# One decoder step on one Trainium2 core: factor sums of the gate and up weights kept in DRAM, sums of the down weights on VectorE, other queues for some transfers

## The chip, the cores and the metric

One core of a Trainium2 chip runs the whole program. The metric is the device time of one execution in microseconds: 2733.95 us is the median of 3 runs (2731.45 to 2736.58).

## The reference

One layer of a hybrid decoder, all in fp32, over 2048 prompt rows and 32 sample rows of width 1024. The change touches only its last part, the feed-forward network:

```python
h2 = rms_norm(x1, norm2_g) * (1.0 + scale2) + shift2
ff = (silu(h2 @ w_gate) * (h2 @ w_up)) @ w_down      # w_gate, w_up: 1024 x 2816, w_down: 2816 x 1024
y = x1 + gate2 * ff
```

Ahead of it come the modulation, the input projection, a dilated attention, a state space and the output projection. Two more outputs are the key and value caches of the 8 samples, moved on by 4 positions: 16 copies of 2044 rows of 2 KB from DRAM to DRAM, one for each cache and sample.

## The kernel before

**How a product is made.** All of the network is in `ffn_parts` (L2473). Each matrix product is done by Strassen's method in Winograd's form: a product of 2x2 quarters as 7 products of sums of quarters instead of 8. For fp32 accuracy each operand is split into a high part (rounded to fp32r, a copy on ScalarE) and a low part (the rest, a subtraction on VectorE), and three matmuls take high x high, high x low and low x high.

**The order of the work on TensorE.** The 2048 rows go in 4 blocks of 512 (`FB`; block 2 also takes the 32 sample rows). In a block, 11 pairs (`NPAIRS`) of column tiles of gate and up weights are taken one after the other, each with 7 products (`PRODUCTS`) of 2 x 12 matmuls (L2860): 1848 matmuls in a block. After blocks 1 and 3 comes the down projection of the last two blocks: 7 products of 11 pieces of 12 matmuls (L2902), 924 matmuls. So the order is block 0, block 1, down 0, block 2, block 3, down 1. In block 3 the 8 matmuls of `sample_parts(n)` (L2872) for the sample rows stand behind product 3 of every pair.

**How weights come in.** SyncE (SP) issues the loads in `load_raw` into a ring of 8 tiles of 128 x 1024 (512 KB, `RAWS`). In a pair of a block there are 4 such tiles, the quarters A21, A22, A11, A12 of the pair's gate and up weights, in packets of 512 bytes. VectorE makes the 4 sums of the pair from them, in place and in `s1` (`weight_sum`, through L3053 and L3045), and does so in all 4 blocks anew. For each product ScalarE (`fill_hi`, L2961) and VectorE (`fill_lo`, L3045) fill one of 4 slots (`SLOTS`) of split weights; slot s+4 is filled once TensorE has let go of slot s. In the down projection a ring tile holds one piece: 512 columns of activation sums (`aF`) and 512 of a weight or weight sum (`w_down`, `wF`). A ring tile is loaded again when the slot made from it is filled (`raw_freed`).

**What GpSimd (POOL) does.** `pool_part` walks through the pairs, waiting for each pair's last product (L3125, L3127 of VectorE). It issues one copy of a cache (`move`, L2731 and L2732) in pairs 1, 4, 6 and 9 of every block. Over blocks 0 and 1 it loads the quarters of `w_down` (`load_quarters`, L2750), makes their 4 sums (`t_sum`, L2746) and stores them (`wF`, L2767), one tile k in 2 pairs. In block 3 it loads the quarters for `sample_parts` into the one buffer `wq`. In blocks 0 and 2 it makes the 4 sums of the next block's activations (L2774). In the down projections it loads rows of `x1` and stores rows of `y_prompt` (`y_dma`, L2742).

**What ScalarE and VectorE do besides.** ScalarE copies product banks out (L2978) and takes SiLU (L2990). VectorE adds products up (L3108), multiplies (L3125) and forms the sums of the activations (`stage_sums`, L3133), which SP stores to `aF` (L2671).

The queue of POOL's transfers is q0, that of SP's and ScalarE's is q1.

Of the kernel before, what the change touches and what calls it, by code (L numbers as in the profile page):

```python
# [7 lines left out]
ALU = mybir.AluOpType  # L8
# [2457 lines left out]
ROUND_RAWS = 2 * PAIR_RAWS * NPAIRS + PIECES  # L2466
# [6 lines left out]
def ffn_parts(nc, t, const, P, M, sig):  # L2473
# [10 lines left out]
    Y_BUF = {C11: 1, C22: 0, C21: 1, C12: 0}  # L2484
    T_AT = {2: 0, 3: 3, 4: 1, 5: 2}
# [3 lines left out]

    def raw_of(b, n, x):  # L2490
        return b // 2 * ROUND_RAWS + (b % 2 * NPAIRS + n) * PAIR_RAWS + x

    def raw_of_piece(r, p, k):
        return r * ROUND_RAWS + 2 * NPAIRS * PAIR_RAWS + p * DEPTH + k

# [5 lines left out]

    def raw_at_index(i):
        r, i = divmod(i, ROUND_RAWS)
        if i < 2 * NPAIRS * PAIR_RAWS:
            g, x = divmod(i, PAIR_RAWS)
            return "pair", 2 * r + g // NPAIRS, g % NPAIRS, x
        return ("piece", r) + divmod(i - 2 * NPAIRS * PAIR_RAWS, DEPTH)
# [55 lines left out]
    s1 = M.at("f_s1", [128, 1024], M.held + 73728)  # L2563
# [6 lines left out]
    wq = M.at("f_wq", [128, 4, 512], M.early + 24576)  # L2570
# [21 lines left out]
    staged, down_copied, wq_moved, t_summed = (P.sem("f_" + v) for v in ("staged", "down_copied", "wq_moved", "t_summed"))  # L2592
# [17 lines left out]

    def load_raw(sp, i):
        dst = raws[i % RAWS]
        kind, *at = raw_at_index(i)
        if kind == "pair":
            _, n, x = at
            k0, col = x % 2 * (KT // 2), (2 * n + (1 if x in (A21, A22) else 0)) * 128
# [32 lines left out]
    def sp_part(sp):  # L2649
# [10 lines left out]
        def raw_freed(i):  # L2660
            kind, *at = raw_at_index(i)
            if kind == "pair":
                b, n, x = at
                sp.wait_ge(w_lo, slot_of(b, n, (4, 5, 3, 6)[x]) + 1)
            else:
                sp.wait_ge(w_lo, slot_of_piece(*at) + 1)

# [13 lines left out]
        def main():  # L2681
# [3 lines left out]
            for i in range(RAW, ROUNDS * ROUND_RAWS):  # L2685
                kind, *at = raw_at_index(i)
# [4 lines left out]
                if kind == "piece":  # L2691
                    r, p, k = at
                    if p == 0:
                        sums_stored(sp, (2 * r + 1) * NPAIRS + k + 1)
                    if p == min(T_AT) and r == 0 and k == 0:
                        sp.wait_ge(wq_moved, 32 * DEPTH)
                load_raw(sp, i)
                if kind == "pair":
                    b, n, x = at
                    if x == A12:  # L2700
                        if b % 2 * NPAIRS + n >= 3:
                            store_sums(b * NPAIRS + n - 3)
                        if b % 2 == 0 and n == 3:
                            load_next(b + 1)
                else:
                    last = (2 * r + 2) * NPAIRS - 1
                    if p == 0 and k in (3, 7, 9):
                        store_sums(last - {3: 2, 7: 1, 9: 0}[k])
# [17 lines left out]
    def pool_part(pool):  # L2726
# [706 lines left out]
```

## Time and profile before

| | |
|---|---|
| median of 3 runs | 2733.95 us |
| profiled execution | 2731.9 us |
| its span, first to last instruction | 2730.1 us |
| mean granted TensorE clock | 0.974 |
| PE, DVE, ACT, POOL busy | 94%, 73%, 47%, 19% |
| moved by the DMA engines | 583.52 MB, mean 214 GB/s |

The network runs from 1284 us to the end. A granted clock of 1.00 is 2.4 GHz, the other level is 1.2 GHz, and a figure between them is a mean over a stretch. The DMA share is the busy time of packets over that of 16 engines; since packets overlap it can be above 1. A copy from DRAM to DRAM counts once in GB/s.

### The profile page before, as it was taken

To read this page: it belongs to the slowest core of one execution; us is meant where nothing else is said; L and a number is where in the kernel's file an instruction comes from. 1 tells how busy PE (TensorE), PEld (TensorE's weight loads), DVE (VectorE), ACT (ScalarE), POOL (GpSimd) and SP (SyncE) were. 2 spreads that over 40 slices of the span, in tenths; PEclk is the share of its full clock that TensorE was granted. 3 is DMA by queue.
4 is the path that set the end of the run, shared out by engine and by line. 5 is a ranking of instruction groups with operands and counts; after the bars stand their busy time and mean duration, and the time that the engine had idled before them with its cause. 6 is when DMAs were issued, how large, how long until landed. Compare 5 with 4: busy or idle time off the path is not lost.

```text
span 2730.1 us, 46745 instructions
## 1 busy us (share of the span) xinstructions
PE 2575.6 (94%) x17757; PEld 2214.9 (81%) x17757; DVE 1983.1 (73%) x3672; ACT 1285.1 (47%) x2509; POOL 507.8 (19%) x632
## 2 busy tenths in 40 slices
PE   5999999999999999998999899989999998888998
PEld 3678887777787778787999899978899997787787
DVE  6657886567767468677999999837698996665546
ACT  4221222247889465665554554535445553443443
POOL 2107787430001000000223121200000100000000
PEclk8999999999999999999999999999999999998999
DMA  9663334753433985445898789787777767766774
GB/s 331 204 191 114 128 119 136 283 175 125 127 110 120 386 320 194 156 151 166 272 312 261 225 266 294 270 273 230 237 218 231 226 195 226 228 210 230 228 225 158
DMA packets 407081, 583.52 MB, mean 214 GB/s; under 512 B 35105, under 2 KB 295969, under 8 KB 396866
## 3 DMA queue, kind: packets, MB, share of 16 engines
q1 hardware_dynamic: 380152, 428.96, 48.9%
q0 software_dynamic: 24256, 150.70, 16.4%
q8 instruction: 142, 2.33, 0.4%
q10 hardware_dynamic: 2450, 0.87, 0.1%
q14 instruction: 81, 0.66, 0.1%
HBM read 447.76 MB, written 199.27 MB: 237 GB/s over the span
## 4 chain that ended last, share of the span: by engine, by line
PE 59%; DVE 8%; DMA 4%; ACT 3%; issue 3%; SPq 1%; POOL 0%; DVEq 0%; ACTq 0%
PE f_ps L2860 23%; PE f_ps L2902 14%; PE c_ps_w L2165 6%; DMA f_wq<-in_w_down_dram 3%; PE a_o_ps L406 2%; PE a_s_ps L377 2%; DVE f_ws L3045 2%; PE a_t_ps L388 2%; PE c_ps_glu L2140 2%; PE b_ps_t L1787 1%; ACT a_probs L444 1%; PE a_o_ps L414 1%; PE b_ps_o L1824 1%; PE b_ps_s L1799 1%; DVE f_s L3053 1%
## 5 line engine op out<-in xcount | busy, mean ns | idle before, releaser
L2860 PEld LDWEIGHTS f_ps<-f_x,f_ws 128*128 128x128 f32 x7392 | 905.2, 191 | 52.1 <-issue 46.1
L2860 PE MATMUL f_ps<-f_x,f_ws 128*128 128x256 f32 (+1 forms) x7392 | 910.7, 286 | 35.6 <-DVE f_sl L3108 22.4
L2902 PE MATMUL f_ps<-f_ws 128*128 128x512 f32 x1848 | 422.9, 391 | 10.6 <-DVE f_ws L3045 10.6
L2902 PEld LDWEIGHTS f_ps<-f_ws 128*128 128x128 f32 x1848 | 347.9, 189 | 85.8 <-DVE f_ws L3045 11.9
L946 PE MATMUL p_out_ps<-p_w,p_hT 128*128 128x512 f32 x1620 | 380.0, 392 | 1.3 <-DVE p_qk L1222 1.1
L946 PEld LDWEIGHTS p_out_ps<-p_w,p_hT 128*128 128x128 f32 x1620 | 300.8, 188 | 73.5 <-issue 11.6
L3045 DVE TENSOR_TENSOR f_ws<-f_raw,f_ws 128x1024 fp32r<-128x1024 f32 x208 | 269.2, 1300 | 124.1 <-ACT f_ws L2961 123.8
L3045 DVE TENSOR_TENSOR f_ws<-raw,f_ws 128x1024 fp32r<-128x1024 f32 x210 | 262.9, 1257 | 115.9 <-ACT f_ws L2961 115.5
L2961 ACT ACTIVATE f_ws<-raw 128x1024 fp32r<-128x1024 f32 x210 | 220.9, 1057 | 208.5 <-PE f_ps L2902 111.2
L2961 ACT ACTIVATE f_ws<-f_raw 128x1024 fp32r<-128x1024 f32 x208 | 218.8, 1057 | 210.8 <-PE f_ps L2902 103.5
L2978 ACT ACTIVATE f_us<-f_ps 128x256 f32<-128x256 f32 (+1 forms) x264 | 100.0, 384 | 205.4 <-PE f_ps L2860 203.6
L444 ACT ACTIVATE a_probs<-a_probs,a_o 128x256 f32<-128x256 f32 (+1 forms) x384 | 171.1, 451 | 1.9 <-DVE a_o L487 1.9
L487 DVE CUSTOM_DVE_ANT_0 a_probs<-a_s_ps,a_mask 128x256 f32<-128x256 f32 (+1 forms) x384 | 117.8, 364 | 60.1 <-issue 59.1
L2165 PE MATMUL c_ps_w<-c_wout_h,c_mT 128*128 128x512 f32 (+1 forms) x544 | 130.8, 397 | 1.8 <-ACT c_mT L2269 1.8
L2165 PEld LDWEIGHTS c_ps_w<-c_wout_h,c_mT 128*128 128x128 f32 (+1 forms) x544 | 98.6, 184 | 27.6 <-ACT c_mT L2269 2.3
L2746 POOL TENSOR_TENSOR f_wq<-f_wq 128x512 f32<-128x512 f32 x44 | 84.4, 1929 | 135.3 <-DVE f_stage L3125 97.7
L863 ACT ACTIVATE p_qk<-p_out_ps 128x1024 f32<-128x1024 f32 (+1 forms) x17 | 17.4, 1024 | 172.4 <-PE p_out_ps L946 172.4
L2990 ACT ACTIVATE f_sl<-f_sl 128x256 f32<-128x256 f32 (+1 forms) x132 | 54.9, 416 | 83.4 <-DVE f_sl L3108 82.3
L3108 DVE TENSOR_TENSOR f_sl<-f_ps,f_us 128x256 f32<-128x256 f32 (+1 forms) x132 | 55.4, 420 | 51.3 <-ACT f_us L2978 51.3
L406 PE MATMUL a_o_ps<-a_probsT,a_v 128*64 128x128 f32 x1200 | 86.7, 281 | 0.2 <-DVE a_probsT L470 0.2
L1216 DVE TENSOR_REDUCE p_hss<-p_qk 128x16 f32<-128x1024 f32 (+1 forms) x17 | 20.7, 1219 | 87.6 <-ACT p_qk L863 87.4
L388 PE MATMUL a_t_ps<-ident,a_probs 128*128 128x128 f32 x600 | 83.9, 277 | 0.2 <-ACT a_probsT L437 0.2
(381 smaller groups left out, 3769.1 us busy)
## 6 DMA issues: line engine op xcount, KB each, us to landing
scratch_aF<-f_stage SPq DMA_DIRECT2D x44, 896.0 KB, 6.6
out_dram<-in_cache_k_dram POOLq DMA_DIRECT2D x8, 4088.0 KB, 14.6
out_dram<-in_cache_v_dram POOLq DMA_DIRECT2D x8, 4088.0 KB, 14.4
raw<-in_w_gate_dram SPq DMA_DIRECT2D x88, 256.0 KB, 5.1
raw<-in_w_up_dram SPq DMA_DIRECT2D x88, 256.0 KB, 5.4
f_raw<-in_w_gate_dram SPq DMA_DIRECT2D x88, 256.0 KB, 4.7
f_raw<-in_w_up_dram SPq DMA_DIRECT2D x88, 256.0 KB, 5.3
f_wq<-in_w_down_dram POOLq DMA_DIRECT2D x22, 1024.0 KB, 7.3
```

Source lines behind the costliest of these rows:

```text
L388: mm = pe.transpose(bank[:, c * QB:(c + 1) * QB], pr[:, n % 2, hd, b * QB:(b + 1) * QB], ident[:, :])
L406: mm = pe.matmul(o_ps[n % 2][e * HD:(e + 1) * HD, pair * QB:(pair + 1) * QB], v[:, (n - (blocks - 1 - b)) % 4, hd * HD:(hd + 1) * HD], prT ...
L444: e = act.activation(pr[:, n % 2, hd, 0:w], pr[:, n % 2, hd, 0:w], ACT.Exp, scale=-1.0, bias=o[:, n % ORING, AW + hd:AW + hd + 1], accum_o ...
L487: mx = dve.tensor_tensor_reduce(pr[:, n % 2, hd, 0:w], s_ps[quad][hd % 2][:, at:at + w], mask[n // BLOCKS][:, 2 * QB - w:], -SCALE, 3e38, ...
L946: mm = pe.matmul(out, hT[:, n % 2, a, k, :], w[b][k][:, c * 512:(c + 1) * 512], start=(k == 0 and i == 0), stop=(k == KT - 1 and i == 2))
L2165: mm = pe.matmul(ps_w[0:r, cols], mT[:, a, k, 0:r], w_out(b, k)[:, cols], start=(i == 0 and k == 0), stop=(i == 2 and k == KT - 1))
L2746: return pool.tensor_tensor(wq[:, out, :], wq[:, left, :], wq[:, right, :], ALU.subtract).then_inc(t_summed, 1)
L2860: mm = pe.matmul(ps[bank][:, 0:w], ws[s % SLOTS][:, y, j * 512 + k * 128:j * 512 + (k + 1) * 128], x_half(b, p, z)[:, k], start=(p < 3 and ...
L2902: mm = pe.matmul(ps[bank][:, :], slot[:, y, j * 128:(j + 1) * 128], slot[:, z, 512:1024], start=(p < 3 and k == 0 and x == 0), stop=(k == ...
L2961: act.activation(ws[s % SLOTS][:, 0], src, ACT.Copy).then_inc(w_hi, 1)
L2978: act.activation(us[:, j, i, 0:w], ps[pair_bank(b, n, "A", j)][:, 0:w], ACT.Copy).then_inc(copied, 1)
L3045: sub = lambda out, x, y: dve.tensor_tensor(out, x, y, ALU.subtract)
```

## The change

- Block 0 works as before, but SP stores the 4 weight sums of each pair to DRAM (`wS`, 4 x 512 KB for a pair). In blocks 1 to 3 the ring gets one tile for each of the 7 products: 3 plain quarters (512-byte packets) and 4 stored sums (2 KB packets). VectorE makes no weight sum there.
- The sums of the down weights are made by VectorE, once for each of 11 tiles, in pairs 1 to 10 of block 1 and in down 0. Their loads and stores, and the loads of the sample's quarters in block 3, go through SP, with 3 buffers `wq` for 1.
- Rows of `x1` and `y_prompt` in the down projections are moved by ScalarE's queue at set pieces.
- The 16 cache copies are respaced: none in block 0; 3 in each of blocks 1 to 3 (pairs 2, 5, 8); 5 in down 0 (at the ends of products 0 to 4) and 2 in down 1.
- `sample_parts(n-1)` stands in pair n, the last one in down 1; the copy of the sample's partial sums and `sample_y` come later.

```diff
+    S_AT = {2: 0, 4: 1, 3: 2, 6: 3}
+    raw_list = [("pair", 0, n, x) for n in range(NPAIRS) for x in range(PAIR_RAWS)]
+    for b in range(1, FB):
+        raw_list += [("factor", b, n, p) for n in range(NPAIRS) for p in range(PRODUCTS)]
+        if b % 2:
+            raw_list += [("piece", b // 2, p, k) for p in range(PRODUCTS) for k in range(DEPTH)]
-    s1 = M.at("f_s1", [128, 1024], M.held + 73728)
+    s1 = [M.at("f_s10", [128, 1024], M.held + 73728), M.at("f_s11", [128, 1024], M.early + 24576)]
-    wq = M.at("f_wq", [128, 4, 512], M.early + 24576)
+    wq = [M.at(f"f_wq{x}", [128, 4, 512], M.held + 81920 + 8192 * x) for x in range(3)]
...
     def load_raw(sp, i):
+        if kind == "factor" and at[2] in S_AT:
+            _, n, p = at
+            for j in range(2):
+                sp.dma_start(dst[:, j * 512:(j + 1) * 512], t["wS"][n, S_AT[p], :, j * 512:(j + 1) * 512]).then_inc(d_raw[i % RAWS], 16)
+        elif kind != "piece":
+            _, n, x = at
+            if kind == "factor":
+                x = {0: A11, 1: A12, 5: A22}[x]
...
         def raw_freed(i):
             if kind == "pair":
                 sp.wait_ge(w_lo, slot_of(b, n, (4, 5, 3, 6)[x]) + 1)
+                if x != A22:
+                    factors_stored(sp, n)
+            elif kind == "factor":
+                sp.wait_ge(w_lo, slot_of(*at) + 1)
+        def store_factors(n):
+            sp.wait_ge(w_sum, 4 * n + 4)
+            for i, src in enumerate((s1[n % 2], *(raws[raw_of(0, n, x) % RAWS] for x in (A21, A11, A12)))):
+                sp.dma_start(t["wS"][n, i], src[:, :]).then_inc(d_ws[n % 2], 16)
...
         def main():        # SP
+                elif kind == "factor":
+                    if p == PRODUCTS - 1:
...
+                        if b == 1 and n >= 3:
+                            store_t(n - 3)
+                        if b == 1 and n >= 1:
+                            load_for_t(n - 1)
+                        if b == 3 and n >= 1:
+                            load_for_sample(n - 1)
                 else:
+                    if r == 0 and (p, k) in ((0, 3), (0, 10), (1, 7)):
+                        store_t({3: 8, 10: 9, 7: 10}[k])
+                    if p == 0 and k == 3:
+                        (load_for_t, load_for_sample)[r](DEPTH - 1)
...
     def pool_part(pool):
-                if n in (1, 4, 6, 9):
-                    move(4 * b + (1, 4, 6, 9).index(n))
-                if r == 0:
-                    t_step(g)
...
+                if b and n in (2, 5, 8):
+                    pool.wait_ge(product, 4 * (b * NPAIRS + n))
+                    move(moved)
+            if b % 2:
+                for p in range(5 if b == 1 else 2):
+                    pool.wait_ge(down, down_end(b // 2, p, 3))
+                    move(moved)
...
     def act_part(act):
+        def y_load(r, c):
+            if c == C11:
+                sums_stored(act, 2 * (r + 1) * NPAIRS)
...
+        Y_STEPS = {(0, 2): (y_load, C11), (0, 4): (y_load, C22), (2, 5): (y_store, C11), (3, 0): (y_load, C21),
+                   (5, 5): (y_store, C22), (6, 0): (y_load, C12), (6, 5): (y_store, C21)}
...
     def dve_part(dve):
-                if p == 0 and g:
-                    weight_sum(g, 1)
+            if kind == "pair" and at[0] == 0:
+                if p == 0 and n:
+                    weight_sum(n, 1)
...
+        def t_sums(k):
+            dve.wait_ge(wq_loaded[k % 2], 16 * (k // 2 + 1))
+            for i, (out, left, right) in enumerate(((0, 1, 0), (1, 3, 1), (3, 3, 0), (2, 2, 3))):
+                sub(q(out), q(left), q(right)).then_inc(t_summed, 1)
+                        if b == 1 and n and p == 4:
+                            t_sums(n - 1)
```

## Rows read from the trace of the kernel before

**Rows 1.** The page: engines' busy time, share of the span, instructions.

```profile
PE 2575.6 (94%) x17757; PEld 2214.9 (81%) x17757; DVE 1983.1 (73%) x3672; ACT 1285.1 (47%) x2509; POOL 507.8 (19%) x632
```

**Rows 2.** Windows of L2860: start:end, us, PE, PEld busy (count), clock, DMA share, GB/s.

```profile
1284.00:1532.00 248.00, 228.42 (x1841) 226.81 (x1842) 0.96 0.90 279
1534.00:1764.10 230.10, 220.72 (x1841) 219.47 (x1839) 0.99 0.84 267
1984.00:2218.00 234.00, 232.46 (x1840) 232.25 (x1841) 1.00 0.76 231
2220.00:2507.40 287.40, 224.94 (x1842) 222.67 (x1840) 0.92 0.69 217
1340.00:1360.00 20.00, 20.00 (x171) 20.00 (x171) 1.00 1.10 339
2040.00:2060.00 20.00, 20.00 (x160) 20.00 (x160) 1.00 1.04 299
```

**Rows 3.** The same windows of L2902, the down projections.

```profile
1763.80:1984.00 220.20, 211.70 (x924) 174.82 (x924) 0.98 0.75 241
2507.00:2722.20 215.20, 210.78 (x924) 173.04 (x924) 1.00 0.64 208
1880.00:1900.00 20.00, 20.00 (x90) 16.57 (x89) 1.00 0.59 181
```

**Rows 4.** PE's waits, 1280 to 2731 us: waiter, releaser, us in total, times, longest.

```profile
PE f_ps L2872 <- DMA f_wq<-in_w_down_dram: 47.6, 5, 11.9
PE f_ps L2860 <- DVE f_sl L3108: 22.4, 13, 4.3
PE f_ps L2902 <- DVE f_ws L3045: 10.6, 3, 8.4
```

**Rows 5.** Timeline of block 3: start us, us, engine, line, instruction [idle before it].

```profile
2378.83 0.53 POOL L2731 DMA_DIRECT2D out_dram<-in_cache_v_dram  x1 [20.35 <-DVE f_stage L3125]
2379.85 0.74 POOL L2750 DMA_DIRECT2D f_wq<-in_w_down_dram  x1
2383.85 10.48 SPq L2619 DMA_DIRECT2D raw<-in_w_up_dram  x1
2397.86 1.94 PE L2872 MATMUL f_ps<-f_wq,f_as 128*32 128x512 f32 x8 [11.12 <-DMA f_wq<-in_w_down_dram]
2420.35 1.07 PE L2872 MATMUL f_ps<-f_wq,f_as 128*32 128x512 f32 x8
```

**Rows 6.** Queues while a cache copy runs, 2325 to 2339 us: packets, MB, share.

```profile
q0 software_dynamic: 143, 4.33, 91.9%
q1 hardware_dynamic: 117, 0.06, 2.2%
```

**Rows 7.** Issues of the cache copies: count, KB each, us to landing.

```profile
out_dram<-in_cache_v_dram POOLq DMA_DIRECT2D x8, 4088.0 KB, 14.4
```

**Rows 8.** DMA totals, 1404 to 1408, 1800 to 1812, 920 to 940 us.

```profile
DMA packets 2346, 1.17 MB, mean 291 GB/s; under 512 B 70, under 2 KB 2346, under 8 KB 2346
...
DMA packets 2553, 4.67 MB, mean 389 GB/s; under 512 B 281, under 2 KB 281, under 8 KB 2552
...
DMA packets 1530, 8.28 MB, mean 414 GB/s; under 512 B 174, under 2 KB 174, under 8 KB 638
```

**Rows 9.** Timeline of block 0, DVE beside POOL's sums, and PE after them.

```profile
1443.88 1.21 DVE L3045 TENSOR_TENSOR f_ws<-f_raw,f_ws 128x1024 fp32r<-128x1024 f32 x1
1445.51 7.99 POOL L2746 TENSOR_TENSOR f_wq<-f_wq 128x512 f32<-128x512 f32 x4 [15.51 <-DVE f_stage L3125]
1445.61 2.27 DVE L3045 TENSOR_TENSOR f_ws<-f_raw,f_ws 128x1024 fp32r<-128x1024 f32 x1 [0.18 <-ACT f_ws L2961]
1450.03 2.31 DVE L3053 TENSOR_TENSOR f_s<-raw 128x1024 f32<-128x1024 f32 x1
1461.77 18.41 PE L2860 MATMUL f_ps<-f_x,f_ws 128*128 128x256 f32 x141 [3.76 <-DVE f_sl L3108]
```

**Rows 10.** DVE groups, down 0 and block 1: count | busy us, mean ns.

```profile
L3173 DVE TENSOR_TENSOR f_yp<-f_yp,f_tmp 128x512 f32<-128x512 f32 x12 | 8.3, 689 | 0.3
...
L3045 DVE TENSOR_TENSOR raw<-raw 128x1024 f32<-128x1024 f32 x10 | 12.2, 1217 | 0.0
```

**Rows 11.** Waits in down 0, and DVE's wait in down 1.

```profile
ACT f_ws L2961 <- DMA f_raw<-in_w_down_dram: 13.1, 1, 13.1
...
POOL f_yp L2742 <- DMA scratch_aF<-f_stage: 17.5, 1, 17.5
...
DVE f_tmps L3179 <- DMA f_ys<-scratch_x: 9.5, 1, 9.5
```

More of the change, by code:

```diff
@@ L2488, in ffn_parts @@
     SAMPLE_BANK = 5
+    raw_list = [("pair", 0, n, x) for n in range(NPAIRS) for x in range(PAIR_RAWS)]
[3 more added lines that the diff above has]
+            raw_list += [("piece", b // 2, p, k) for p in range(PRODUCTS) for k in range(DEPTH)]
+    raw_index = {x: i for i, x in enumerate(raw_list)}
     def raw_of(b, n, x):
-        return b // 2 * ROUND_RAWS + (b % 2 * NPAIRS + n) * PAIR_RAWS + x
+        return raw_index[("pair" if b == 0 else "factor", b, n, x)]
     def raw_of_piece(r, p, k):
-        return r * ROUND_RAWS + 2 * NPAIRS * PAIR_RAWS + p * DEPTH + k
+        return raw_index[("piece", r, p, k)]
     def slot_of(b, n, p):
@@ L2684, in main @@
             all_stored(sp, x1_stored)
-            for i in range(RAW, ROUNDS * ROUND_RAWS):
-                kind, *at = raw_at_index(i)
+            for i in range(RAW, len(raw_list)):
+                kind, *at = raw_list[i]
                 if i == RAWS - 1:
@@ L2915, in pe_part @@
                         merge["last_turn"]()
-                    if b == SAMPLE_BLOCK + 1 and p == 3:
-                        sample_parts(n)
+                    if b == SAMPLE_BLOCK + 1 and n >= 1 and p == 3:
+                        sample_parts(n - 1)
             if b % 2:
@@ L2950, in act_part, with y_dma, y_store @@
     def act_part(act):
+        def y_dma(r, c, out):
+            buf = Y_BUF[c]
+            cols = slice(QUARTER[c][1] * 512, (QUARTER[c][1] + 1) * 512)
+            for x in range(2):
+                at = y_row(r, c, 2 * x)
+                name, sem = ("y_prompt", d_y) if out else ("x1", d_x)
+                far = t[name][at:at + 256, cols].rearrange("(j p) n -> p j n", p=128)
+                near = yp[buf][:, 2 * x:2 * x + 2, :]
+                act.dma_start(far if out else near, near if out else far).then_inc(sem[buf], 16)
+        def y_load(r, c):
+            if c == C11:
+                if r == 0:
+                    all_stored(act, x1_stored)
+                sums_stored(act, 2 * (r + 1) * NPAIRS)
+            if c == C22 and r == 0:
+                for n in (NPAIRS - 2, NPAIRS - 1):
+                    factors_stored(act, n)
+                act.wait_ge(w_lo, slot_of(0, NPAIRS - 1, 2) + 1)
+            before = 64 * r + (32 if c in (C21, C12) else 0)
+            if before:
+                act.wait_ge(d_y[Y_BUF[c]], before)
+            y_dma(r, c, False)
+        def y_store(r, c):
+            act.wait_ge(added, y_added(r, c, 3))
+            y_dma(r, c, True)
+        Y_STEPS = {(0, 2): (y_load, C11), (0, 4): (y_load, C22), (2, 5): (y_store, C11), (3, 0): (y_load, C21),
+                   (5, 5): (y_store, C22), (6, 0): (y_load, C12), (6, 5): (y_store, C21)}
         def fill_hi(s):
@@ L3245, in main @@
                         summed_y(r, c, k)
[L3246 to L3247 removed]
+                    if r == ROUNDS - 1 and p == 0 and k in (8, 10):
+                        sample_y((k - 8) // 2)
                     if r + 1 < ROUNDS and X_AT <= i < X_AT + 11:
```

204 lines of the change are left out of this document (95 added, 109 removed).

## The prediction

> **What bounds the kernel now.** I read the page's busy times first, then the waits of TensorE, then windows with one stage each, then the timeline around the longest waits. TensorE is busy 94% of the span [rows 1], so only its pauses and its slow stretches are to be had. The full pace is 171 matmuls of 256 columns in 20 us (0.117 us each), 160 of 272 columns (0.125 us), and 90 of 512 columns (0.222 us) [rows 2, 3]. With 1848 matmuls in a block and 924 in a down projection the floors are 216 us for blocks 0, 1 and 3, 230 us for block 2 and 205.5 us for a down projection. The stages' own lengths, carried from the counts in the windows to full 1848, are:
>
> - block 0: 248 us, 32 over its floor
> - block 1: 231 us, 15 over
> - down 0: 220 us, 15 over
> - block 2: 234.5 us, 4.5 over
> - block 3: 289 us, 73 over, of which 12 are the sample's own 88 matmuls (11 groups of 1.07 us at full clock [rows 5]); 61 remain
> - down 1: 215 us, 2 of them for two folding matmuls, so 7 over [rows 2, 3]
>
> The waits put names to it. TensorE waits 47.6 us in 5 turns for `f_wq` from DRAM, all in block 3; 22.4 us in 13 turns for VectorE's add-ups; 10.6 us for VectorE's split weights [rows 4]. In block 3 the clock was 0.92 over the stage [rows 2]: after a pause of some 11 us the first matmuls run at the lower level, 1.94 us for a group that takes 1.07 us [rows 5]. That is how 47.6 us of waiting become some 61.
>
> The cause of the long waits is in the timeline. POOL issues a 4 MB cache copy at 2378.83 and the sample's quarters at 2379.85 behind it, and TensorE stands at them until 2397.86 [rows 5]. While a copy runs its queue has 91.9% of the engines and SP's queue 2.2%, 0.06 MB in 14 us [rows 6], and a copy takes 14.4 us [rows 7]. So I count a cache copy as 14.4 us in which no other transfer moves.
>
> **Part 1: the sample's quarters through SP with three buffers (block 3).** The load for pair n is issued behind the last ring tile of that pair, and tile 8 behind is what frees it: TensorE is then in pair n-1, about 9 products of 2.8 us (25 us) ahead of the matmuls that use it. A copy in between costs 14.4 us, a landing some 7 more. The wait is covered, and with it goes the slow clock. I take 57 of the 61 us. Bounds: all 61, or 45 if the new load on the queue (part 3) brings pauses back.
>
> **Part 2: VectorE and POOL.** One group of 4 sums on POOL takes 8 us; beside it a VectorE subtraction of two SBUF tiles takes 2.27 and 2.31 us for 1.21 [rows 9]. VectorE is some 6 us behind afterwards, and TensorE waits 3.76 us for an add-up [rows 9]. 11 groups go. In block 0 the 15 us over the floor before 1320 us belong to the end of the stage ahead and to the first activation sums and stay; of the other 17 I keep 4, for the activation sums that POOL still makes and for seven `x_lo` in the last pair. Gain 13 us, bounds 5 and 20. From block 1 on VectorE loses 33 x 4 weight sums of 1.217 us (161 us) and gets 44 sums of 128x512, priced by the nearest row at 0.689 us (30 us) [rows 10]. In block 1 that is 5 us less and 2.8 us more in a pair of 20: VectorE is off the path there, and its last-pair backlog in block 2 (half of 4.5 us) goes too: 2 us.
>
> Block 0 also gets new waits: SP stands at `store_factors(n-1)` until VectorE's last sum of that pair, and the next quarters wait until 2 MB are stored (some 9 us). The quarters so delayed have about 28 us until `weight_sum` needs them. Cost nothing; if VectorE falls behind, up to 5 us.
>
> **Part 3: what it costs in transfers.** This is the term that works against the change. The trace gives three rates of a full queue: 291 GB/s with packets of about 500 bytes, 389 GB/s at about 1.8 KB, 414 GB/s at about 5.4 KB [rows 8]. For the 1 KB packets of `aF` and of activations I take 320 GB/s, between the first two. Then, in us of DMA time with nothing else:
>
> - Block 0: weights 23.1 MB / 291 = 79; stores of sums 21 MB / 414 = 51; `aF` 7.3 MB and activations 3.7 MB / 320 = 34. Sum 164 of 216. No copies now. Not a bound.
> - Block 1: 33 plain tiles 17.3 MB / 291 = 59.5; 44 stored sums 23.1 MB / 389 = 59.4; 12 `aF` stores 11 MB / 320 = 34; quarters in 10.5 and sums out 8.4 MB / 414 = 46; 3 copies 43. Sum 242 of 216. Bound.
> - Down 0: 77 pieces 40.4 MB / 389 = 104; rows of `x1` and `y_prompt` 7.3 MB / 389 = 19; activations and `aF` 5.7 MB / 320 = 18; rest of the down sums 4.2 MB / 414 = 10; 5 copies 72. Sum 223 of 205.5. Bound until the last product.
> - Block 2: 119 + 29 + 12 + 3 + 43 = 206 of 230. Not a bound.
> - Block 3: 119 + 32 + 25 + 43 = 219 of 228. Just not.
> - Down 1: some 165 of 205. Not a bound.
>
> Set against the trace of before, the same count for its block 1 (79 + 34 + 28 + four copies 58 = 199 of 231) is 0.86, and the DMA share there is 0.84 [rows 2], so the count holds. Block 1 and down 0 hang together, since a late tile of one is the late start of the other. Up to the end of product 5 of down 0 the transfers need 242 + 223 - 18 = 447 us; some 10 of these may be done ahead in the ring (8 tiles) at the start; then comes one product at TensorE's 29.4 us: 466 us. Before, both took 451. I take 15 us more. Bounds: if transfers of two queues overlap and nothing starves, TensorE's floor plus 7 for the start of down 0, 429, so 22 less; if the mean rate is worse, much more (first rival).
>
> The Trainium skill speaks against the change here: "SBUF — State Buffer", in its bandwidth table, gives a core some 358 GB/s to HBM, below two of my three rates. By it the 121 MB that go through in these two stages beside the copies would take 338 us instead of the 332 I count, and the sum would be about 6 us higher. The rows with 389 and 414 GB/s do not agree with it [rows 8], so I keep them.
>
> **Part 4: rows through ScalarE's queue.** ScalarE stands at `y_load` at piece 2 of down 0 until the last `aF` store has landed. Before, POOL stood there 17.5 us [rows 11], until 10 us after the stage's start. Queued behind the wait are ScalarE's fills; TensorE has slots up to piece 6 and needs the next about 16 us after the start. Covered by 6 us, or a few us late with a full queue; this is in the 466. The later steps come two pieces after what they wait for. Down 0 also keeps its old pause: 3.9 MB of activations ahead of the pieces, ScalarE 13.1 us late [rows 11]; it too is in the transfer count. In down 1 VectorE waits 9.5 us for `f_ys` in front of its fills [rows 11]; `sample_y` now comes 5 pieces later: 3 us gained, 0 to 5. `sample_parts` only moves.
>
> **Sum.** -13 (block 0) +15 (block 1 and down 0) -2 (block 2) -57 (block 3) -3 (down 1) = -60. The profiled execution took 2731.9 us, so 2672; the median of the runs shown is 2 us above it, so 2674.
>
> **Rivals.**
>
> *The transfers become the bound of half the network* (slower). One ring tile per product doubles the requests and the queue never gets past the 291 GB/s of small packets, because plain tiles alternate with stored sums. Block 1: 70.3 MB / 291 + 43 = 285. Down 0: 57.6 / 291 + 72 = 270. Less 23 for the last product's transfers and 10 ahead, plus 29: 551 against 451, +100. Block 3: 61 / 291 + 43 = 253, -36. With -13, -2 and -3: +46, 2780 us. It decides from where the mean rate beside the copies falls below about 315 GB/s (121 MB / 315 = 384 us, +115 for 8 copies, +19 = 518: +67, which eats the rest). For it: share above 1 in many windows of before, and SP held for 10.48 us at one issue [rows 5]. Against: the 389 GB/s.
>
> *The transfers are hidden.* Two queues overlap and the ring evens it out: -17, -22, -4, -61, -4 = -108, 2626 us. For it: windows at 1.10 [rows 2]. Against: 2.2% beside a copy [rows 6].
>
> *The copies bite in the ring.* Now every product needs a tile of its own, so 8 tiles last 22 us, and a copy (14.4) and the `aF` and quarter transfers behind it (6 to 9) use that up. Each of the 14 copies before down 1 then costs TensorE some 4 us at the lower clock, where it was free: on the 6 of blocks 2 and 3 that is 24, on the other 8 half of it in addition to the bound, 16. -60 + 40: 2714 us.
>
> *Nothing to be seen:* gains and losses cancel, 2734 us.
>
> **Chances.** Forecast (2655 to 2700) 0.50; hidden 0.17; copies bite 0.16; slower 0.13; none 0.04. Faster by over 0.2% (5.5 us, about what can be told from no change) 0.83, within it 0.03, slower 0.14. The range reaches from the hidden case to the lower part of the slower one: 2625 to 2745.
>
> **What would show it.** Right: no wait of L2872 for `f_wq` and 228 to 235 us in block 3; block 0 near 235 us with no DVE subtraction above 1.3 us but beside POOL's four; block 1 and down 0 together 455 to 480 us, DMA share near 1, with TensorE's pauses ending on ScalarE's fills that waited for `raw` or `f_raw`. Wrong: block 1 near 217 us (hidden), or pauses a fixed time behind every copy in blocks 2 and 3 (copies bite), or block 1 above 260 us (bound). Pauses of ScalarE at `y_load` longer than 10 us would make part 4 wrong.

## The result and the profile after

The kernel after takes 2715.5 us (median, 2708.3 to 2720.2), the kernel before 2734.0: ratio 0.9929, 95% interval 0.9908 to 0.9951. It is faster, by 18 us where 60 were forecast (2674). The number lies at the third rival's 2714, whose mechanism is only partly what happened, as the experiments show.

The page after, busy times and the line on DMA packets:

```profile
PE 2575.1 (95%) x17757; PEld 2219.4 (82%) x17757; DVE 1832.6 (67%) x3584; ACT 1286.5 (47%) x2509; POOL 379.3 (14%) x525
...
DMA packets 420425, 658.51 MB, mean 242 GB/s; under 512 B 38977, under 2 KB 266049, under 8 KB 410210
```

VectorE lost 150 us of work, POOL 128 [rows 1]. Yet only block 3 became shorter. The windows after, one for each stage (block 0, block 1, down 0, block 2, block 3, down 1); start:end, length, then PE, PEld, DVE, ACT, POOL busy (count), clock, DMA share, GB/s:

```profile
1286.30:1543.10 256.80, 230.15 (x1845) 229.16 (x1846) 212.52 (x285) 129.88 (x202) 11.29 (x6) 0.93 0.78 247
1543.10:1784.00 240.90, 224.69 (x1861) 224.17 (x1860) 173.86 (x273) 117.38 (x188) 3.06 (x6) 0.97 1.01 344
1784.00:2019.40 235.40, 211.73 (x926) 174.87 (x926) 133.11 (x136) 93.12 (x96) 4.92 (x10) 0.95 0.96 334
2019.40:2257.60 238.20, 233.47 (x1833) 233.24 (x1832) 163.70 (x277) 122.86 (x192) 12.51 (x10) 0.99 0.88 280
2257.60:2490.30 232.70, 232.70 (x1947) 222.98 (x1947) 154.38 (x241) 118.60 (x190) 2.99 (x6) 1.00 0.98 323
2490.30:2710.00 219.70, 216.30 (x938) 175.50 (x937) 118.27 (x123) 84.82 (x88) 1.96 (x4) 0.98 0.72 240
```

Against the stages of before (measured in the same way: 248.6, 231.0, 220.3, 234.6, 288.6, 214.7) block 3 gained 56 us, and every other stage lost: 8, 10, 15, 4 and 5 us. With 2 us from a later start the last matmul ends 12 us earlier than before. (The profiled execution of after took 2720.2 us, the longest of its five; hence 12 here and 18 between medians.)

TensorE's waits after, 1280 to 2731 us (waiter, releaser, us in total, times, longest), to be set against [rows 4]:

```profile
PE f_ps L2874 <- ACT f_us L3028: 26.2, 5, 9.8
PE f_ps L2916 <- DVE f_ws L3099: 23.7, 1, 23.7
PE f_ps L2874 <- DVE f_sl L3170: 14.3, 2, 9.3
PE f_ps L2874 <- issue: 7.0, 2, 4.9
PE f_ps L2874 <- DVE f_x L3099: 7.0, 1, 7.0
PE f_ps L2916 <- DVE f_tmps L3241: 3.4, 1, 3.4
```

The 47.6 us for `f_wq` are gone. Block 3 now runs at an even step, as its timeline shows (`L2886` is the sample's matmul, `L2872` of before); compare the 11.12 us pause and the 1.94 us group of [rows 5]:

```profile
2292.15 20.14 PE L2874 MATMUL f_ps<-f_x,f_ws 128*128 128x256 f32 x168
2312.22 1.07 PE L2886 MATMUL f_ps<-f_wq,f_as 128*32 128x512 f32 x8
2313.22 20.14 PE L2874 MATMUL f_ps<-f_x,f_ws 128*128 128x256 f32 x168
```

In their place stand few but long pauses elsewhere. Block 0, timeline: VectorE's waits and the TensorE pauses that follow them.

```profile
1316.06 1.23 DVE L3110 TENSOR_TENSOR f_s<-f_raw,f_raw 128x1024 f32<-128x1024 f32 x1 [10.41 <-DMA scratch_h2T<-c_h2T]
...
1376.12 1.21 SPq L2714 DMA_DIRECT2D scratch_aF<-f_stage  x1
...
1384.43 0.43 DVE L3187 TENSOR_TENSOR f_stage<-f_sl,f_cu 128x256 f32<-128x256 f32 x1 [7.18 <-DMA scratch_aF<-f_stage]
1388.75 4.61 PE L2874 MATMUL f_ps<-f_x,f_ws 128*128 128x256 f32 x20 [5.09 <-DVE f_sl L3170]
...
1534.80 0.43 DVE L3187 TENSOR_TENSOR f_stage<-f_sl,f_cu 128x256 f32<-128x256 f32 x1 [9.96 <-DMA scratch_aF<-f_stage]
1540.25 3.11 PE L2874 MATMUL f_ps<-f_x,f_ws 128*128 128x256 f32 x13 [9.25 <-DVE f_sl L3170]
```

VectorE does not lack time at these places: it waits. Until 1316 the first weight sum of pair 1 waits for the last store of `h2T`, because `all_stored` asks for all of them. Later `multiply` waits for the `aF` store that still holds its stage buffer. SP issues that store (L2714) behind the 2 MB of `store_factors`. The store behind the second wait, that of pair 8, is also placed 3 tiles later in the pair than before and goes out at 1526.66; in before it went out at 1511.51.

Block 1, the longest of three pauses. All three end 20 to 35 us after a copy is issued, and each time a fill of ScalarE has waited for a ring tile:

```profile
1642.46 2.15 SPq L2709 DMA_DIRECT2D scratch_wF<-f_wq  x1
1644.71 0.80 SPq L2689 DMA_DIRECT2D f_wq<-in_w_down_dram  x1
...
1650.70 0.52 POOL L2802 DMA_DIRECT2D out_dram<-in_cache_k_dram  x1 [60.45 <-DVE f_stage L3187]
...
1651.29 11.85 SPq L2629 DMA_DIRECT2D f_raw<-in_w_up_dram  x1
...
1669.26 1.06 ACT L3011 ACTIVATE f_ws<-f_raw 128x1024 fp32r<-128x1024 f32 x1 [10.74 <-DMA f_raw<-in_w_up_dram]
...
1670.73 3.54 PE L2874 MATMUL f_ps<-f_x,f_ws 128*128 128x256 f32 x15 [9.79 <-ACT f_us L3028]
```

Down 0, the single pause of 23.67 us: SP is in the middle of the activations, the copy goes out, and the pieces are queued behind both.

```profile
1814.50 0.51 POOL L2802 DMA_DIRECT2D out_dram<-in_cache_k_dram  x1 [91.33 <-PE f_ps L2916]
...
1816.90 10.67 SPq L2648 DMA_DIRECT2D f_xf<-scratch_h2T  x1
...
1835.45 1.06 ACT L3011 ACTIVATE f_ws<-f_raw 128x1024 fp32r<-128x1024 f32 x1 [25.59 <-DMA f_raw<-in_w_down_dram]
...
1837.87 4.47 PE L2916 MATMUL f_ps<-f_ws 128*128 128x512 f32 x10 [23.67 <-DVE f_ws L3099]
```

Block 2 and down 1, one pause each. In block 2 `load_next(3)` comes behind a copy. In down 1 the second half of the moved `sample_y` reads the bank that product 1 needs, and TensorE waits for this read (L3241):

```profile
2065.10 0.50 POOL L2802 DMA_DIRECT2D out_dram<-in_cache_v_dram  x1 [104.01 <-DVE f_as L3189]
...
2079.18 13.30 SPq L2645 DMA_DIRECT2D f_xn<-scratch_h2T  x7
...
2103.08 7.08 PE L2874 MATMUL f_ps<-f_x,f_ws 128*128 128x272 f32 x36 [4.74 <-ACT f_us L3028]
...
2528.90 3.35 PE L2916 MATMUL f_ps<-f_ws 128*128 128x512 f32 x7 [3.40 <-DVE f_tmps L3241]
```

### The profile page after: what moved, and what is told of

It reads as the page before. It is cut to its first block, busy times and chain, and to the rows that moved or that the text cites. A ratio compares the mean times of both kernels' runs of the same rounds, so it can differ in the third digit from the quotient of the medians.

```text
span 2718.1 us, 46863 instructions
## 1 busy us (share of the span) xinstructions
PE 2575.1 (95%) x17757; PEld 2219.4 (82%) x17757; DVE 1832.6 (67%) x3584; ACT 1286.5 (47%) x2509; POOL 379.3 (14%) x525
## 4 chain that ended last, share of the span: by engine, by line
PE 65%; DMA 4%; SPq 3%; ACT 3%; DVE 2%; issue 1%; DVEq 0%; ACTq 0%
PE f_ps L2874 28%; PE f_ps L2916 14%; PE c_ps_w L2165 6%; PE a_s_ps L377 3%; PE a_o_ps L406 2%; PE a_t_ps L388 2%; PE c_ps_glu L2140 2%; PE b_ps_t L1787 1%; DMA scratch_aF<-f_stage 1%; ACT a_probs L444 1%; PE a_o_ps L414 1%; DMA raw<-in_w_up_dram 1%; SPq L2645 1%; DMA f_raw<-in_w_up_dram 1%; PE b_ps_s L1799 1%
## 5 line engine op out<-in xcount | busy, mean ns | idle before, releaser
L2916 PE MATMUL f_ps<-f_ws 128*128 128x512 f32 x1848 | 425.6, 392 | 27.1 <-DVE f_ws L3099 23.7
L3099 DVE TENSOR_TENSOR f_ws<-f_raw,f_ws 128x1024 fp32r<-128x1024 f32 x223 | 276.1, 1242 | 215.1 <-ACT f_ws L3011 214.8
L3099 DVE TENSOR_TENSOR f_ws<-raw,f_ws 128x1024 fp32r<-128x1024 f32 x228 | 283.6, 1248 | 176.0 <-ACT f_ws L3011 175.2
L3011 ACT ACTIVATE f_ws<-f_raw 128x1024 fp32r<-128x1024 f32 x223 | 234.9, 1058 | 276.0 <-PE f_ps L2874 116.2
L3011 ACT ACTIVATE f_ws<-raw 128x1024 fp32r<-128x1024 f32 x228 | 240.1, 1057 | 239.3 <-PE f_ps L2874 115.5
L377 PE MATMUL a_s_ps<-a_kW,a_qT 64*128 64x256 f32 (+1 forms) x512 | 77.6, 422 | 0.0
L406 PEld LDWEIGHTS a_o_ps<-a_probsT,a_v 128*64 128x64 f32 x1200 | 63.5, 136 | 16.3 <-issue 15.8
```

What stands on the lines that cost most here:

```text
L377: mm = pe.matmul(bank[:, at:at + blocks * QB], turned_q, keys(kW, half, pair, n, blocks), start=True, stop=True)
L406: mm = pe.matmul(o_ps[n % 2][e * HD:(e + 1) * HD, pair * QB:(pair + 1) * QB], v[:, (n - (blocks - 1 - b)) % 4, hd * HD:(hd + 1) * HD], prT ...
L2916: mm = pe.matmul(ps[bank][:, :], slot[:, y, j * 128:(j + 1) * 128], slot[:, z, 512:1024], start=(p < 3 and k == 0 and x == 0), stop=(k == ...
L3011: act.activation(ws[s % SLOTS][:, 0], src, ACT.Copy).then_inc(w_hi, 1)
L3099: sub = lambda out, x, y: dve.tensor_tensor(out, x, y, ALU.subtract)
```

## The experiments

All stage lengths below come from TensorE's timeline, from the first matmul of a stage to the end of its 1848th (924th in a down projection). b0 to b3 are the blocks, D0 and D1 the down projections. "us" is the median of all executions, while the stages are those of the profiled one. The ratio is over all executions, to executions of the kernel before taken beside them, with its 95% interval; so two kernels with one median can differ a little in it (after and e11).

| kernel | b0 | b1 | D0 | b2 | b3 | D1 | us | ratio |
|---|---|---|---|---|---|---|---|---|
| before | 248.6 | 231.0 | 220.3 | 234.6 | 288.6 | 214.7 | 2734.0 | |
| after | 256.8 | 240.9 | 235.4 | 238.2 | 232.7 | 219.7 | 2715.5 | 0.9929 (0.9908-0.9951) |
| e1_swap | 248.0 | 228.1 | 220.4 | 234.7 | 241.5 | 215.8 | 2683.4 | 0.9824 (0.9804-0.9845) |
| e2_nocopy | 256.4 | 220.9 | 221.9 | 231.2 | 232.3 | 219.6 | 2677.5 | 0.9796 (0.9777-0.9815) |
| e3_block0 | 232.2 | 236.9 | 235.8 | 237.5 | 232.7 | 218.2 | 2687.0 | 0.9834 (0.9818-0.9850) |
| e4_copies | 254.8 | 241.5 | 223.6 | 231.2 | 232.3 | 219.6 | 2698.2 | 0.9873 (0.9857-0.9889) |
| e5_wait | 249.5 | 237.6 | 236.2 | 236.0 | 232.5 | 219.5 | 2705.1 | 0.9901 (0.9884-0.9917) |
| e6_order | 238.3 | 236.2 | 236.1 | 236.2 | 232.5 | 216.8 | 2690.7 | 0.9852 (0.9837-0.9867) |
| e7_nosums | 251.1 | 231.8 | 220.0 | 234.7 | 244.1 | 215.8 | 2684.1 | 0.9832 (0.9814-0.9850) |
| e8_best | 230.9 | 219.5 | 223.1 | 231.2 | 232.3 | 213.1 | 2644.5 | 0.9680 (0.9666-0.9695) |
| e9_nocopy | 246.6 | 227.8 | 220.9 | 234.7 | 236.5 | 214.4 | 2676.2 | 0.9794 (0.9780-0.9809) |
| e10_neither | 233.6 | 219.5 | 219.4 | 234.7 | 236.6 | 215.0 | 2654.9 | 0.9715 (0.9701-0.9730) |
| e11_half | 254.4 | 241.7 | 237.8 | 234.1 | 232.3 | 218.4 | 2715.8 | 0.9955 (0.9936-0.9974) |
| e12_best2 | 231.5 | 220.1 | 211.9 | 231.2 | 232.3 | 213.1 | 2635.4 | 0.9647 (0.9633-0.9661) |
| e13_spread | 255.8 | 240.5 | 236.6 | 235.9 | 232.5 | 219.4 | 2713.2 | 0.9936 (0.9917-0.9956) |

**e1_swap.** The kernel before; in block 3 the sample's quarters go out ahead of the copy on POOL's queue.

```diff
-                if n in (1, 4, 6, 9):
+                if n in (1, 4, 6, 9) and b < FB - 1:
                     move(4 * b + (1, 4, 6, 9).index(n))
...
                         load_quarters(n)
+                    if n in (1, 4, 6, 9):
+                        move(4 * b + (1, 4, 6, 9).index(n))
```

> The kernel before, with one exchange: in block 3 POOL issues the sample's quarters ahead of the cache copy that it issued first. If the 47.6 us of waits in block 3 came only from standing behind the copy in one queue (my theory), block 3 falls from 289 to about 232 us and the whole to about 2680 us (-54), with nothing else of the change. If any transfer next to a copy is late (rival), the quarters land late still, the waits stay near 11 us each, and the time stays within 10 us of 2734.

Block 3 fell from 288.6 to 241.5 us and the time to 2683.4. So the order of two issues on one queue was the cause of the long waits, and this exchange alone brings 51 us, almost three times what the whole change brings. What is left of the wait, in TensorE's waits of this kernel:

```profile
PE f_ps L2874 <- DMA f_wq<-in_w_down_dram: 6.5, 4, 3.0
```

**e2_nocopy.** The kernel after without the cache copies (the 4 MB part of each `move`).

```diff
-            pool.dma_start(t[out][s, 0:PAST - TS, :], t[src][s, TS:PAST, :]).then_inc(d_m, 16)
...
-        pool.wait_ge(d_m, 16 * 4 * NB)
+        pool.wait_ge(d_m, 16 * 2 * NB)
```

> The changed kernel without the 16 large cache copies (their rows are not written; the small copies of 4 rows stay). If the pauses of 9.8 us in block 1, 23.7 us in down 0 and 4.7 us in block 2 come from copies that meet a bulk of other transfers, they go: block 1 about 218, down 0 about 221, block 2 about 231, together -45, and block 0 stays at 258; about 2668 us. If the volume of the stored sums is the bound (rival), the ring's pauses stay in block 1 and the time falls by less than 20 us.

Block 1, down 0 and block 2 fell by 20, 13.5 and 7 us (a pause of 10.7 us stays in down 0); blocks 0 and 3 and down 1 did not move. So after's copies cost some 40 us, all of it in three stages. Block 3, with three copies at a DMA share of 0.98, pays nothing: a copy in a full stage is not dear by itself.

**e3_block0, e5_wait, e6_order.** The kernel after with two edits to block 0's waits: e5 is the first diff, e6 the second, e3 both.

```diff
-                    all_stored(dve, h2_stored)
+                    dve.wait_ge(h2_stored[1], 16 * (TILES_C // 2))
```
```diff
-                        if n:
-                            store_factors(n - 1)
                         if n >= 3:
                             store_sums(n - 3)
+                        if n:
+                            store_factors(n - 1)
...
                     if b == 1 and n == 0 and p == 2:
+                        store_sums(g - 3)
                         store_factors(NPAIRS - 1)
-                    if b == 1 and n == 1 and p == 2:
-                        store_sums(g - 3)
                     if p == PRODUCTS - 1:
                         if b == 1 and n == 0:
-                            store_sums(g - 3)
+                            store_sums(g - 2)
```

> The changed kernel with block 0 mended only: SP issues each store of activation sums ahead of the stores of weight sums (and those of pairs 8 and 9 one step sooner), and VectorE's wait in pair 1 is for the one buffer that shares memory with it, not for the last tile's store. If block 0 lost its gain to these two (my theory), the pauses of 9.3, 5.1 and about 10 us there shrink, block 0 goes from 258 to about 238 us and the whole to about 2695 us. If block 0 is held by the 23 MB of stores as such (rival), VectorE's waits for a stored buffer stay and the time moves less than 6 us.

> The changed kernel with one wait made exact: VectorE's first use of the second sum buffer waits only for the store that reads the same memory, not for the last tile's store as well. My theory: the 10.4 us wait of VectorE at 1306 goes, TensorE's pauses at 1309 and 1319 (10 us together) shrink to about 4, block 0 goes from 257 to about 250: about 2709 us (-7). Rival: the wait was covered by others behind it, less than 2 us.

> The changed kernel with SP's stores of activation sums ahead of the weight sums' stores, and those of pairs 8 and 9 one step sooner. The whole mend of block 0 gave 28 us, more than the 19 us of its named pauses and half clock. My theory: the order is the larger part, the pauses at 1389 and 1540 go, block 0 goes from 257 to about 240: about 2698 us (-17). Rival: the two parts hold each other and this one alone gives less than 8 us, because the ring runs late from the start of the block.

Block 0: 256.8 with neither, 249.5 with the wait shortened, 238.3 with the order, 232.2 with both. The parts add up (7.3 + 18.5 = 25.8, both 24.6). Block 1 gained another 4 us in e3. Block 0 is then 3 us below the 235 forecast for it. So the forecast's saving on VectorE was there to be had; two waits that the change adds took it and 8 us more.

**e4_copies.** The kernel after; copies and `load_next(3)` moved, none left out.

```diff
-                        if b == 2 and n == 3:
+                        if b == 2 and n == 4:
...
-                    pool.wait_ge(product, 4 * (b * NPAIRS + n))
+                    pool.wait_ge(made, product_end(b * NPAIRS + n, 3, 1))
...
-                for p in range(5 if b == 1 else 2):
+                for p in range(1, 6) if b == 1 else range(2):
```

> The changed kernel with the copies placed elsewhere only: in blocks 1 to 3 they are issued after product 3 of a pair in place of its start, in down 0 at the ends of products 1 to 5 in place of 0 to 4, and block 3's activations are loaded one pair later. If place decides (my theory), the pauses of 9.8 us in block 1 and 4.7 us in block 2 go and that of down 0 shrinks from 23.7 to about 9 us: about 2685 us (-30). If a copy costs its 14.4 us of transfers wherever it stands (rival), the pauses move with it and the time stays within 6 us of 2715.

Down 0 fell to 223.6 and block 2 to 231.2, within 2 us of what they take without copies: there the *place* of a copy cost the time. (In block 2 the copy and `load_next(3)` were moved at once, so this does not say which of the two shifts did it.) Block 1 stayed at 241.5, though its pause of 9.8 us was expected to go: half a pair's shift does nothing there.

**e7_nosums, e9_nocopy, e10_neither.** The kernel before. e7 is e1 with POOL's quarter sums left out (`t_sum`, `t_summed` out of `t_step`); e9 has no 4 MB copies (the diff of e2); e10 has neither, without the exchange.

> The kernel before with the exchange in block 3 (quarters ahead of the copy) and without POOL's 44 sums of the down weights: the quarters are stored as they are. It prices what those sums cost. My theory: VectorE is slowed by them, block 0 goes from 248 to about 235 and block 1 from 228 to about 219, in all about 2661 us (-22 on the run with the exchange alone). Rival: TensorE's 13 short waits come from VectorE's own load of weight sums, and less than 8 us go.

> The kernel before without the 16 large cache copies (their rows are not written), POOL's sums kept. Leaving the sums out alone moved nothing and VectorE waited 36 us for the store of activation sums instead. My theory now: in blocks 0 and 1 either cause alone makes TensorE wait, the sums by slowing VectorE, the copies by holding that store. Then here block 3 falls to about 232 and block 1 to about 226 because of the sums: about 2672 us, with VectorE's slow subtractions still there. Rival: the sums cost nothing in any case, and blocks 0 and 1 reach 233 and 219 already here.

> The kernel before without the large cache copies and without POOL's sums of the down weights (quarters stored as they are). Two causes that hide each other (my theory): with both gone block 0 is about 236 and block 1 about 219, 14 us or more below the kernel with only the copies out: about 2657 us. Rival, VectorE's own weight sums bound these blocks: within 5 us of the kernel with only the copies out.

Blocks 0 and 1 together take 476 us in e1, 483 without the sums, 474 without the copies, 453 without either. The 483 come from an execution that took 8.5 us more than the median of e7; by the medians e7 (2684.1) equals e1 (2683.4), so the sums alone are worth nothing, and not minus 7. The expectation of e7 (22 us from the sums) was wrong. VectorE was indeed fast again in e7, but it waited, as its waits from 1320 to 1766 us show:

```profile
DVE f_stage L3120 <- DMA scratch_aF<-f_stage: 36.4, 9, 6.2
```

The `aF` store is late there because a copy of 14.4 us [rows 7] runs in front of it: in e9 and e10, without the copies, VectorE has no wait of this kind from 1320 to 1766 us. Without copies it was POOL's sums that held VectorE back (groups of VectorE in e9, 1320 to 1500 us; busy, mean ns; alone the first takes 1210 ns [rows 9]):

```profile
L3044 DVE TENSOR_TENSOR f_ws<-f_raw,f_ws 128x1024 fp32r<-128x1024 f32 x27 | 38.1, 1410 | 6.1 <-ACT f_ws L2960 6.1
...
L3052 DVE TENSOR_TENSOR f_s<-raw 128x1024 f32<-128x1024 f32 x5 | 11.6, 2317 | 0.0
```

The second group shows it plainly. In e10, without the sums, it is at its own speed:

```profile
L3045 DVE TENSOR_TENSOR f_s<-raw 128x1024 f32<-128x1024 f32 x5 | 6.1, 1216 | 0.0
```

The first group doesn't: its mean is still 1310 ns in e10, for POOL's sums of activations fall into the same stretch.

Two causes stood behind one loss, and each was enough for most of it. The prediction booked the 13 us to the sums alone. With both gone (e10) blocks 0 and 1 of before run at these windows:

```profile
1286.30:1519.90 233.60, 224.94 (x1856) 224.27 (x1857) 215.52 (x286) 129.07 (x202) 21.06 (x21) 0.98 0.74 224
1519.90:1739.40 219.50, 218.94 (x1851) 218.77 (x1850) 194.58 (x279) 117.30 (x188) 9.01 (x15) 1.00 0.68 208
```

That is within 3 us of e8's block 0 and equal to its block 1, with VectorE busy for 195 of 220 us. The stored weight sums, the part that adds the traffic, bring VectorE's work in block 1 down to 174 us in after, where TensorE was not waiting for it; over blocks 0, 1 and 2 e8 is 6 us ahead of e10, with down 0 between them 2.5 us. What the stored weight sums are worth by themselves is therefore not shown: e10 has no quarter sums and no copies at all, so it is no exact undoing of that part, and none was run.

**e8_best.** e3, `load_next(3)` at n 4, no copy in block 1 (5 in each down projection, 3 in blocks 2 and 3), and the sample's two adds two pieces earlier.

```diff
-                if b and n in (2, 5, 8):
+                if b > 1 and n in (2, 5, 8):
...
-                for p in range(5 if b == 1 else 2):
+                for p in range(1, 6) if b == 1 else range(5):
...
-                    if r == ROUNDS - 1 and p == 0 and k in (8, 10):
-                        sample_y((k - 8) // 2)
+                    if r == ROUNDS - 1 and p == 0 and k in (7, 8):
+                        sample_y(k - 7)
```

> The changed kernel with all mends: block 0's order and exact wait, no copy in block 1 and none at the end of product 0 of down 0 (5 copies at the ends of products 1 to 5 there, 3 in block 2, 3 in block 3, 5 in down 1), block 3's activations loaded one pair later, and the sample's rows added after pieces 7 and 8 of down 1 in place of 8 and 10. My theory, by stages: 232 + 221 + 224 + 231 + 232.5 + 215, about 2651 us. Rival, if a copy costs transfers wherever it stands: the pauses move to down 1, which rises from 219 to over 225, and the whole stays above 2662 us.

2644.5 us. Block 1 is at 219.5 with the copies out of it, down 1 at 213.1 though it took three more: where the DMA share is low (0.72 in after) they cost nothing that can be seen. With the earlier add the pause of 3.4 us in down 1 is gone, and the stage is 6.6 us shorter than in after; no run has this add alone, and e6, without it, already has 216.8.

**e11_half.** The kernel after, with only the first 64 partitions of each stored sum loaded (the matmuls read old data in the rest).

```diff
-                sp.dma_start(dst[:, j * 512:(j + 1) * 512], t["wS"][n, S_AT[p], :, j * 512:(j + 1) * 512]).then_inc(d_raw[i % RAWS], 16)
+                sp.dma_start(dst[0:64, j * 512:(j + 1) * 512], t["wS"][n, S_AT[p], 0:64, j * 512:(j + 1) * 512]).then_inc(d_raw[i % RAWS], 16)
```

> The changed kernel with each stored weight sum loaded for 64 of 128 partitions (the other half of the tile is left as it was), so 11.5 MB less in each of blocks 1 to 3, copies in place. If volume and copies act together in block 1 (my theory), its pauses shrink and it falls from 241 to about 225; down 0 stays at 235 because its pause comes from the activations and the copy; block 2 falls from 238 to about 233: about 2693 us. If a copy alone does it (rival), block 1 stays above 236 and the time above 2706.

Block 1 did not move (241.7). This was meant as the test of volume, and the expectation from volume (2693) is missed by 23 us. But it is not a clean test. The DMA view of block 1, for e11 (1541 to 1783 us) and then for after (1543 to 1784 us): totals; the share of SP's queue in the engines' time; the loads of stored sums, KB each and us to landing:

```profile
DMA packets 52612, 72.69 MB, mean 300 GB/s; under 512 B 2977, under 2 KB 41592, under 8 KB 51245
...
q1 hardware_dynamic: 52253, 59.80, 83.1%
...
f_raw<-scratch_wS SPq DMA_DIRECT2D x42, 128.0 KB, 5.6
```
```profile
DMA packets 57527, 82.83 MB, mean 344 GB/s; under 512 B 2960, under 2 KB 41536, under 8 KB 56160
...
q1 hardware_dynamic: 57168, 69.94, 86.4%
...
f_raw<-scratch_wS SPq DMA_DIRECT2D x42, 256.0 KB, 5.3
```

10 MB fewer took only 3.3% of 241 us, 8 us, from the engines' time, and half a tile landed no sooner than a whole one. So e11 takes away bytes and hardly any transfer time, and leaves the question of volume open.

**e13_spread.** The kernel after, block 1's quarter store and load behind two different products instead of together behind the last, each one pair later.

```diff
-                        if b == 1 and n >= 3:
-                            store_t(n - 3)
-                        if b == 1 and n >= 1:
-                            load_for_t(n - 1)
...
+                    if b == 1 and n >= 4 and p == 1:
+                        store_t(n - 4)
+                    if b == 1 and n >= 2 and p == 3:
+                        load_for_t(n - 2)
...
+                    if r == 0 and (p, k) == (0, 0):
+                        store_t(7)
+                        load_for_t(9)
```

> The changed kernel with block 1's stores and loads of down sums (1 MB each) issued behind the tiles of products 1 and 3 of the pair, one pair later, and no longer both behind product 6 with the store of activation sums; copies in place. Half the volume of stored sums left block 1 at 241.7 us, so volume alone is not it. If it is 3 MB in one bulk in front of the ring just as a copy starts (my theory), the pauses of 9.8 and 4.8 us go and block 1 falls from 241 to about 225: about 2700 us. If a copy beside any such load is enough (rival), block 1 stays above 236 and the time above 2710.

Block 1 stayed at 240.5, but the pauses are not the same ones. TensorE now waits for VectorE's `multiply` (L3190), and VectorE stands in front of it, in its sums of the down weights, waiting for the quarters. Its waits in block 1 and the longest place:

```profile
DVE f_wq L3102 <- DMA f_wq<-in_w_down_dram: 27.4, 4, 12.2
...
1670.18 2.87 DVE L3102 TENSOR_TENSOR f_wq<-f_wq 128x512 f32<-128x512 f32 x4 [12.24 <-DMA f_wq<-in_w_down_dram]
...
1673.77 2.50 PE L2877 MATMUL f_ps<-f_x,f_ws 128*128 128x256 f32 x10 [8.52 <-DVE f_stage L3190]
```

In after VectorE never waits for `f_wq` in block 1. The quarters, loaded one pair later, come too late when a copy runs in front of them. So the edit brought a wait of its own, and e13 does not tell whether the bulk behind product 6 was the cause.

**e12_best2.** e8 with the seven parts of block 2's activations loaded one by one between the pieces of down 0.

```diff
+        X_PARTS = {(1, 2): B11, (1, 4): B21, (1, 6): T1, (1, 8): T2, (1, 10): B22, (2, 0): T4, (2, 2): T3}
...
+                    if r + 1 < ROUNDS and (p, k) in X_PARTS:
+                        load_next(2 * r + 2, (X_PARTS[p, k],))
...
                         if r + 1 < ROUNDS:
-                            load_next(2 * r + 2)
+                            pass
```

> The version at 2644 us with one more step: the 7 parts of block 2's activations are loaded one by one between pieces of products 1 and 2 of down 0 and not all in front of piece (1, 0). My theory: down 0's last pause, 10.7 us at 1776 and the slow clock after it, is the ring standing behind 3.9 MB; it goes, and down 0 falls from 223 to about 209: about 2631 us. Rival: the pause comes from the full queue of block 1's end (stores of activation sums, down sums), and stays above 5 us.

2635.4 us, the best version: 3.5% below before, 80 us below after. The pause of 10.7 us that e8 still had in down 0 is gone. Its windows of block 1 and down 0:

```profile
1515.40:1735.50 220.10, 220.10 (x1863) 220.10 (x1862) 174.72 (x275) 118.20 (x189) 0.00 (x0) 1.00 1.02 331
1735.50:1947.40 211.90, 209.87 (x927) 173.28 (x926) 132.30 (x135) 93.03 (x96) 5.05 (x10) 1.00 0.99 349
```

TensorE never pauses in block 1, in down 0 for 2 us, at DMA shares of 1.02 and 0.99. Block 1 has no copy here, and SP's queue alone takes more of the engines' time than in after (86.4% for 69.94 MB, above):

```profile
q1 hardware_dynamic: 60276, 72.63, 101.6%
```

Down 0 carries all its transfers and five copies and is 23.5 us shorter than in after.

## Why the prediction was off, step by step

- **Part 1, block 3: right.** -57 forecast, -56 measured. The wait for `f_wq` and the slow clock behind it both went. By e1, 47 of the 56 come from the order of two issues and do not need SP or the three buffers.
- **Part 2, block 0: the step that failed most.** Forecast -13, measured +8: 21 of the 48 us between forecast and trace. The failing sentence is "Cost nothing; if VectorE falls behind, up to 5 us". It followed SP's wait to the quarters behind it, but not to the `aF` store behind it, whose buffer `multiply` needs two pairs on, and it left out `all_stored` ahead of the first weight sum. e6 and e5 price them at 18.5 and 7.3 us. The 13 us themselves were also credited to POOL's sums alone, where the copies hid behind them (e7, e9, e10).
- **Part 3, block 1 and down 0: +15 forecast, +25 measured.** Counted as pure DMA time block 1 came to 242 and took 240.9, and e2 and e8 confirm that the copies make it long (20 us for three). The size fits, but whether by more than luck stays open. The count's own test was that it gave 0.86 for block 1 of before, where the DMA share was 0.84; in block 1 of e12 it gives 199 us of 220, 0.90, and the share is 1.02, so the share does not confirm it. e4 moved the copies by half a pair without effect; e11 and e13 are no clean tests. What makes a copy cost 7 us here and nothing in block 3 is not shown. In down 0 the count was the wrong model, and this is the second step that failed ("Bound until the last product"): the stage is 211.9 us with every transfer in it (e12). Its 15 us are one pause, 23.7 us where the longest of before was 8.4 [rows 4], from a copy in the middle of 3.9 MB of activations (e4, copy moved: stage -12; e12, loads spread: another -11 against e8). The prediction named the activations "in the transfer count" and so gave no place to them.
- **Block 2: "Not a bound", and -2.** It was not bound by volume, but `load_next(3)` came behind a copy: +4 (e4, which moves both, gives 7 back, and so does e2).
- **Down 1: -3 forecast, +5 measured.** The later `sample_y` cleared the fills, but its second half now comes after piece 10, and the bank that it reads is one that product 1 needs: TensorE waits 3.4 us for it. With it two pieces up (e8) that wait is gone: 213.1 us, less than before.
- **Part 4: right.** ScalarE idled 2.84 us before its first fill behind `y_load`, where 10 us would have been the sign against it.

Of the rivals, the copies that bite had the number, 2714, by luck: it puts 24 us on blocks 2 and 3, 4 for each copy, where block 3's three cost nothing and block 2 has one bad place, and it keeps the -13 for block 0. In block 1 the copies cost more, 7 us each. The slower rival needed a mean rate under 315 GB/s; block 1 moved its 70.3 MB beside the copies in 241 - 43 us, at 355, if a copy stops all others as counted, and without copies at 331 with TensorE never waiting (e12). The hidden rival's block 1 of 217 is come near (219.5 in e8) only with the copies elsewhere.

## What to carry to other kernels

When a step is moved on a queue, write down everything now queued behind it and follow each to the buffer it frees, not only the transfer the step was about; here the stores put in front of another cost 18 us. A DMA total says whether a stage can hold its transfers, but pauses come from places: a burst of loads with a copy in it cost TensorE 24 us, and 2 us with the loads spread and the copy one product later. Before crediting a loss to one cause, take out its neighbour as well: two causes each large enough show little or nothing when removed singly (476 us, then 483 and 474, and 453 with both gone). And after an experiment that changes nothing, look whether the old pauses are still there or new ones stand in their place, as in e13.

## What the hardware showed unexpectedly

DMA engines at a share of 1 do not mean a starved TensorE: 220 us at 1.02 and 212 us at 0.99 ran almost without a pause (e12). Two windows of 20 us of after, at the end of block 3 and in down 0:

```profile
2460.00:2480.00 20.00, 20.00 (x171) 19.32 (x164) 13.18 (x21) 10.38 (x17) 0.00 (x0) 1.00 1.05 382
1920.00:1940.00 20.00, 20.00 (x90) 16.57 (x89) 9.21 (x8) 10.55 (x12) 0.98 (x2) 1.00 1.09 409
```

These are 382 and 409 GB/s, TensorE busy throughout; the second window holds 3.07 MB of a cache copy from 1930 us on, the first holds none. The Trainium skill's "SBUF — State Buffer" gives a core some 358 GB/s to HBM in its bandwidth table; the measurement decides, here as in [rows 8]. And a load of half the partitions, 64 with 128 KB, took 5.6 us to land (e11) beside 5.3 us for all 128 with 256 KB (after).
